# RG-LRU gates of a hybrid decoder layer: both gates of a block from one 64x128 stationary, in pairs on the row halves, with the turned prompt rows and a silu in other places

## What is computed

```
xc, conv_new = _causal_conv(xa, conv0, conv_w, conv_b)
xb = xc.reshape(B, L, N_BLK_A, BLK_A)                       # 8 blocks of 64
r = sigmoid(einsum('blnc,ncd->blnd', xb, wa).reshape(B, L, D_A) + ba)
i = sigmoid(einsum('blnc,ncd->blnd', xb, wx).reshape(B, L, D_A) + bx)
log_a = -8 * softplus(-lam) * r
u = sqrt(max(-expm1(2 * log_a), 0)) * (i * xc)
h = scan(h_t = exp(log_a) * h_{t-1} + u)
ya = h * silu(ga)
```

## Time and profile before

| | before |
|---|---|
| median of 3 runs | 942.91 us (942.79 to 1157.3) |
| the profiled execution: time | 940.88 us |
| its span, first to last instruction | 939.2 us |
| mean granted clock of TensorE | 0.985 of 2.4 GHz |
| PE busy | 872.4 us, 93% |
| DVE busy | 677.3 us, 72% |
| ACT busy | 511.4 us, 54% |
| POOL busy | 266.0 us, 28% |
| chain of work that ended last | PE 60%, DVE 18%, ACT 9%, issue 7%, POOL 3%, DMA 2% |

### The profile page before, as it was taken

One profiled execution on the slowest core, in us unless ns is written; L12 is line 12 of the kernel. 1 busy time (PEld: TensorE's weight loads), 2 busy tenths in 40 slices (PEclk: granted clock), 3 DMA queues, 4 the chain that ended last, 5 costly groups with the idle time before them and its releaser, 6 DMA issues.

```text
span 939.2 us, 20896 instructions
## 1 busy us (share of the span) xinstructions
PE 872.4 (93%) x8151; PEld 639.7 (68%) x8151; DVE 677.3 (72%) x1784; ACT 511.4 (54%) x1057; POOL 266.0 (28%) x348
## 2 busy tenths in 40 slices
PE   5788958999999999999999999999999999999884
PEld 4647847469665977588756866597757865686742
DVE  3577876757786887767785878678776778576865
ACT  2664658536663566547753566356653764346541
POOL 6041256503241223213140324122321314032400
PEclk9999988999999999999999999999999999999998
DMA  9975111301110102010110111010200001010414
GB/s 359 386 303 223 46 45 46 113 1 68 46 56 14 69 1 91 23 43 28 45 69 1 68 46 48 21 68 2 90 24 30 17 1 54 1 46 2 130 68 125
DMA packets 24703, 68.55 MB, mean 73 GB/s; under 512 B 3164, under 2 KB 12208, under 8 KB 20124
## 3 DMA queue, kind: packets, MB, share of 16 engines
q1 hardware_dynamic: 24604, 67.20, 19.7%
HBM read 56.24 MB, written 10.95 MB: 72 GB/s over the span
## 4 chain that ended last, share of the span: by engine, by line
PE 60%; DVE 18%; ACT 9%; issue 7%; POOL 3%; DMA 2%; SPq 0%; DVEq 0%; ACTq 0%; POOLq 0%
PE ring L450 48%; DVE xc L1392 6%; DMA work<-in_ada_w_dram 2%; DVE qlo L1295 2%; DVE kk L1313 2%; POOL wol L1807 2%; PE okv L547 1%; PE okv L549 1%; PE okv L548 1%; ACT wih L1059 1%; DVE qq L1311 1%; PE aux L569 1%; DVE xc L1390 1%; ACT qhi L939 1%; ACT L1002 1%
## 5 line engine op out<-in xcount | busy, mean ns | idle before, releaser
L450 PE MATMUL ring<-hnh,wih 128*128 128x256 bf16 (+1 forms) x1152 | 288.9, 262 | 2.2 <-DVE hnl L1440 2.2
L450 PE MATMUL ring<-hnl,wih 128*128 128x256 f16 (+1 forms) x1152 | 288.8, 262 | 0.0
L450 PE MATMUL ring<-hnh,wil 128*128 128x256 bf16 (+1 forms) x1152 | 288.8, 262 | 0.0
L450 PE MATMUL ring<-woh,work 128*128 128x512 f16 x512 | 164.7, 382 | 6.8 <-ACT sil L969 6.7
L1820 POOL TENSOR_TENSOR klo<-kk,khi 128x256 bf16<-128x256 f32 x96 | 75.5, 786 | 223.9 <-ACT khi L935 223.5
L450 PEld LDWEIGHTS ring<-hnh,wih 128*128 128x128 f16 x1152 | 109.9, 98 | 14.0 <-DVE hnl L1440 2.8
L450 PEld LDWEIGHTS ring<-hnl,wih 128*128 128x128 f16 x1152 | 109.8, 98 | 12.0
L450 PEld LDWEIGHTS ring<-hnh,wil 128*128 128x128 bf16 x1152 | 109.8, 98 | 11.6
L1295 DVE TENSOR_TENSOR qlo<-qq,qhi 128x256 f16<-128x256 f32 x112 | 66.6, 595 | 70.8 <-ACT qhi L939 61.3
L450 PE MATMUL ring<-wih,hnh 128*128 128x512 f16 x256 | 97.1, 379 | 2.4 <-ACT kk L918 1.3
L450 PE MATMUL ring<-wol,work 128*128 128x512 bf16 x256 | 97.7, 382 | 0.0
(11 more groups left out here) (366 smaller groups left out, 1899.5 us busy)
## 6 DMA issues: line engine op xcount, KB each, us to landing
work<-in_x_prompt_dram SPq DMA_DIRECT2D x16, 512.0 KB, 3.2
out_dram<-work SPq DMA_DIRECT2D x16, 512.0 KB, 2.6
xin<-in_x_turned_dram SPq DMA_DIRECT2D x7, 1024.0 KB, 4.8
xs<-in_x_prompt_dram SPq DMA_DIRECT2D x26, 256.0 KB, 3.8
work<-in_ada_w_dram SPq DMA_DIRECT2D x4, 1024.0 KB, 8.0
woh<-in_ada_w_dram SPq DMA_DIRECT2D x4, 1024.0 KB, 14.2
wol<-in_w_in_dram SPq DMA_DIRECT2D x4, 1024.0 KB, 13.6
work<-in_w_in_dram SPq DMA_DIRECT2D x4, 1024.0 KB, 10.3
```

What stands on the lines that cost most here:

```text
L450: last = mm(out, a(k), b(k), start=start and k == ks[0] and j == 0, stop=stop and k == ks[-1] and j == 2)
```

## The change

Both gates of a 64-channel block stand side by side in one 64x128 stationary: for the even block of a tile (rows 0 to 63) r left and i right, for the odd block (rows 64 to 127) i left and r right. A call of `gates` is four matmuls as before, of 64 rows each, neighbours on different row halves; the even blocks' results go to `aux[0]` and the odd blocks' to `aux[1]`, and one signal `g_ps` takes the place of two. There are no zeros left to write, so POOL's zeroing goes. Each sigmoid becomes two of 64 partitions; for i the source and the result lie on different partition halves. The decode's gates and sigmoids change in the same way. On PE the turned rows go behind the Q projection, the FR and Q projections wait for `esq` (the squares that free the ring banks) instead of the gate sigmoids, and `turn_k(n,1)` waits for the i sigmoids instead of the r ones. On ACT the second silu goes ahead of the root of half 0.

```
             def gates(n, p):
                 pe.wait_ge(cvc.sem, cvc.at(n, 8 * p + 8))
-                for w, s in ((0, gr_ps), (1, gi_ps)):
-                    ...
-                    for c in range(2):
-                        last = mm(aux[(1 + w + p) % 2][:, T * c:T * c + T], wg[:, w, 2 * p + c, :], xc[:, p, c, :],
-                                  start=True, stop=True)
-                    last.then_inc(s.sem, 1)
+                if p == 0:
+                    if n == 0:
+                        pe.wait_ge(wg_ld, 64)
+                        pe.wait_ge(gate_ok, 1)
+                    else:
+                        pe.wait_ge(ytl.sem, ytl.at(n - 1, 4))
+                else:
+                    pe.wait_ge(i_sig.sem, i_sig.at(n, 2))
+                if p == 0 and n < BODIES - 1:
+                    pe.wait_ge(xn_ok, NT + n + 1)
+                pe.wait_ge(kt_sb.sem, kt_sb.at(n, p + 1))
+                for c in range(2):
+                    for odd in range(2):
+                        k = slice(HALF * odd, HALF * odd + HALF)
+                        last = mm(aux[odd][:, T * c:T * c + T], wg[k, 2 * p + c, :], xc[k, p, c, :], start=True, stop=True)
+                last.then_inc(g_ps.sem, 1)
...
                 weights(1)
-                if not first:
-                    pe.wait_ge(i_sig.sem, i_sig.at(n - 1, 4))
+                if n == 1:
+                    pe.wait_ge(gp_sb, 2)
+                elif n > 1:
+                    pe.wait_ge(esq[0].sem, esq[0].at(n - 2, 2))
                 project(ring[0], FR, 0, n)
                 project(ring[0], FR, 1).then_inc(fr_ps.sem, 1)
+                weights(2)
+                if n > 1:
+                    pe.wait_ge(esq[1].sem, esq[1].at(n - 2, 2))
+                project(ring[1], Q_, 0)
+                project(ring[1], Q_, 1).then_inc(q_ps.sem, 1)
                 if not first:
                     turn_y(n - 1, 0)
                     turn_y(n - 1, 1)
-                weights(2)
-                project(ring[1], Q_, 0)
-                project(ring[1], Q_, 1).then_inc(q_ps.sem, 1)
...
             def gates_out(n, p):
-                act.wait_ge(gr_ps.sem, gr_ps.at(n, p + 1))
+                act.wait_ge(g_ps.sem, g_ps.at(n, p + 1))
                 act.wait_ge(iu.sem, iu.at(n, p))
                 for c in range(2):
-                    A(rr[:, c, :], aux[(1 + p) % 2][:, T * c:T * c + T], ACT.Sigmoid,
-                      bias=pcol("ba", 2 * p + c)).then_inc(r_sig.sem, 1)
-                act.wait_ge(gi_ps.sem, gi_ps.at(n, p + 1))
+                    for odd in range(2):
+                        k, src = slice(HALF * odd, HALF * odd + HALF), aux[odd][:, T * c:T * c + T]
+                        ins = A(rr[k, c, :], src[k, :], ACT.Sigmoid, bias=pcol("ba", 2 * p + c)[k, :])
+                    ins.then_inc(r_sig.sem, 1)
                 act.wait_ge(scan.sem, scan.at(n, 2 * p))
                 for c in range(2):
-                    A(ii[:, c, :], aux[p][:, T * c:T * c + T], ACT.Sigmoid, bias=pcol("bx", 2 * p + c)).then_inc(i_sig.sem, 1)
+                    for odd in range(2):
+                        k, o = slice(HALF * odd, HALF * odd + HALF), slice(HALF * (1 - odd), HALF * (1 - odd) + HALF)
+                        ins = A(ii[k, c, :], aux[odd][o, T * c:T * c + T], ACT.Sigmoid, bias=pcol("bx", 2 * p + c)[k, :])
+                    ins.then_inc(i_sig.sem, 1)
...
                 heads(n, 1, 7)
+                ga_out(n, 1)
                 root(n, 0)
-                ga_out(n, 1)
...
-            G.memset(wg[:, :, :, :], 0.0).then_inc(zeroed, 1)
```

More of the change, by code:

```diff
@@ L41 @@
 P = 128
+HALF = P // 2
 D = 1024
@@ L116, in build @@
         sil = sb("sil", [P, CT, T])
-        wg = sb("wg", [P, 2, CT, P])
+        wg = sb("wg", [P, CT, P])
         qq = sb("qq", [P, 2 * T])
@@ L184, in build @@
         u_ps = Signal("u_ps", 4)
-        gr_ps, gi_ps = Signal("gr_ps", 2), Signal("gi_ps", 2)
+        g_ps = Signal("g_ps", 2)
         f_sig, k_sig, q_sb = Signal("f_sig", 2), Signal("k_sig", 2), Signal("q_sb", 2)
@@ L367, in _ @@
                 if (kind, c) == ("ada", 7):
-                    sp.wait_ge(zeroed, 1)
                     for w, src in ((0, rg_wa), (1, rg_wx)):
@@ L371, in _ @@
                             v = src[0].rearrange("(t two) c d -> two c t d", two=2)[odd]
-                            sp.dma_start(wg[64 * odd:64 * odd + 64, w, :, 64 * odd:64 * odd + 64], v).then_inc(wg_ld, 16)
+                            col = HALF * (w ^ odd)
+                            sp.dma_start(wg[HALF * odd:HALF * odd + HALF, :, col:col + HALF], v).then_inc(wg_ld, 16)
             def residual_in(n, t):
@@ L503, in turn_y @@
                     pe.wait_ge(yb_ok.sem, yb_ok.at(n, 8))
-                    pe.wait_ge(r_sig.sem, r_sig.at(n, 4))
-                else:
                     pe.wait_ge(i_sig.sem, i_sig.at(n, 4))
@@ L553, in gates @@
                 pe.wait_ge(cvc.sem, cvc.at(n, 8 * p + 8))
-                for w, s in ((0, gr_ps), (1, gi_ps)):
[L555 to L565, removed]
-                    else:
-                        pe.wait_ge(i_sig.sem, i_sig.at(n, 2))
-                    for c in range(2):
-                        last = mm(aux[(1 + w + p) % 2][:, T * c:T * c + T], wg[:, w, 2 * p + c, :], xc[:, p, c, :],
-                                  start=True, stop=True)
-                    last.then_inc(s.sem, 1)
+                if p == 0:
+                    if n == 0:
+                        pe.wait_ge(wg_ld, 64)
+                        pe.wait_ge(gate_ok, 1)
+                    else:
+                        pe.wait_ge(ytl.sem, ytl.at(n - 1, 4))
[9 more added lines that the diff above has]
+                last.then_inc(g_ps.sem, 1)
             def ada(i, bank):
@@ L726, in body @@
                 if last_body:
-                    pe.wait_ge(r_sig.sem, r_sig.at(n, 2))
                     pe.wait_ge(i_sig.sem, i_sig.at(n, 2))
@@ L776, in _ @@
             turn_mod(3, ring[1], 0)
-            pe.wait_ge(zeroed, 3)
+            pe.wait_ge(zeroed, 2)
             pe.wait_ge(carry_zero, 2)
@@ L854, in _ @@
             pe.wait_ge(dv("conv_d"), 16)
[L855 to L858, removed]
+            for c in range(CT):
+                for hf in range(2):
+                    k = slice(HALF * hf, HALF * hf + HALF)
+                    last = mm((lev[1], aux[0])[hf][:, TD * c:TD * c + TD], wg[k, c, :], xcd[k, TD * c:TD * c + TD],
+                              start=True, stop=True)
             last.then_inc(dv("gates_ps"), 1)
@@ L1216, in _ @@
                 for c in range(CT):
-                    o = W4 * w + TD * c
-                    A(dst[:, TD * c:TD * c + TD], lev[1][:, o:o + TD], ACT.Sigmoid, bias=pcol(bias, c)).then_inc(dv("ri_d"), 1)
+                    cols = slice(TD * c, TD * c + TD)
+                    for hf in range(2):
+                        k, o = slice(HALF * hf, HALF * hf + HALF), HALF * (hf ^ w)
+                        ins = A(dst[k, cols], (lev[1], aux[0])[hf][o:o + HALF, cols], ACT.Sigmoid, bias=pcol(bias, c)[k, :])
+                    ins.then_inc(dv("ri_d"), 1)
             act.wait_ge(dv("ri_d"), 2 * CT)
@@ L1621, in _ @@
             rest(2)
-            dve.wait_ge(zeroed, 3)
+            dve.wait_ge(zeroed, 2)
             body(0, True, False)
```

## The result

The changed kernel takes 974.23 us (median of four runs, 970.93 to 977.17) against 942.85 us of the kernel before on the same chip. The ratio is 1.034, with a 95% interval of 1.030 to 1.038: slower, and outside the range of 932 to 957. The profiled execution took 977.17 us, its span is 975.5 us, and the mean granted clock of TensorE was 0.965 instead of 0.985.

The account below looks back on a forecast made before the run. It took a body's chain to run over TensorE, and over DVE and ACT in the last quarter. Body 0 to 1 +1.0, six bodies +3.0, last body and decode +1.5 sum to +5.5 us: 948.4, range 932 to 957.

Parts of the forecast that it names:

- Sigmoids on ACT: Gate sigmoids on ACT: eight halves start 0.36 us apart like whole ones, so a call grows 1.44 us; bounds 0 and 2.3.
- Rival E: Half sigmoids on ACT don't overlap: +2.3 us a call, level 0 at +1.4, 955 and up to 960 us; chance 0.07.
- Rival D: TensorE waits of about 2 us at level 7, over 1 at level 0 lower its clock: 966 us; chance 0.04.
- Level 7 is the first place that gives: Second pass's last level on TensorE, behind DVE's masked copy: 0.2 us slack, begins 1.35 us later, waits about 2 us.
- Level 0 is the second: Next body's first level on TensorE, behind DVE's `qrl`: 0.8 us slack, begins 0.5 us later each body, six times +3.0.
- The silu's wait goes for good: TensorE's wait for the second silu: 1.13 us goes with silu ahead of root, but level 7's +1.35 leaves +0.2.
- Gates in pairs run side by side: Gate matmuls on TensorE: 1.73 us a call becomes 0.87; saves 0.87, or about 0.67 with mode changes, lost in waits.
- Turned rows and looser waits cost nothing and gain nothing by themselves: Turned rows after Q and looser `esq` waits: no cost or gain; without them FR would wait for the longer sigmoids.
- The two ends: Body 0 to 1: +1.0 us. Last body and decode: +1.5 us together, +0.6 at decode input and +0.9 for sixteen sigmoids.

Follow-up runs that it names:

- pairs, grouped halves, rows ahead: Changed kernel with four half sigmoids writing partitions 0 to 63, then four writing 64 to 127, and ring[0]'s twelve output-row matmuls ahead of level 7: 961.27 us, ratio 1.020.
- the grouped halves: Changed kernel with only the half sigmoids reordered: four that write partitions 0 to 63, then four that write 64 to 127: 967.88 us, ratio 1.028.

## Why the prediction was wrong

The lengths of a middle body carry the account. The second column is the time from one call's first sigmoid to the instruction behind the last, the third the start of two level 0s that follow each other.

| kernel | sigmoids of a call | level 0 to level 0 | a body |
|---|---|---|---|
| before | 1.44 us | 579.76 to 681.75 | 101.99 us |
| + silu first | 1.44 | 574.73 to 675.43 | 100.70 |
| + turned rows behind Q | 1.44 | 574.54 to 675.22 | 100.68 |
| + pairs, whole sigmoids | 1.44 | 573.18 to 673.27 | 100.09 |
| pairs, halves all on one half | 2.87 | 586.39 to 688.74 | 102.35 |
| pairs, grouped halves, rows ahead | 3.38 | 588.64 to 692.44 | 103.80 |
| changed, clock at 1.00 | 3.92 | 711.22 to 816.09 | 104.87 |
| changed, clock falls | 3.92 | 604.83 to 711.22 | 106.39 |

From 101.99 to 106.39: -1.29 for the silu, -0.02 for the turned rows, -0.59 for the pairs, +4.78 for the halves, +1.52 for the clock. Behind level 7 the clock falls in five of the six middle bodies, at 1.5 to 1.7 us each. In the profiled execution, whose span is 36.3 us longer than before, the six bodies take 28.7 us more: six times 2.88 = 17.3 for the halves less the gains, about 8.2 for these five falls, 1.7 for one more behind level 0 of body 1, and 1.5 in the body from 390.22 to 498.30, where ACT waits 1.56 us for a DMA (at 405.35). The rest is 3.7 us ahead of them and 4.0 behind. The halves alone (4.78 a body) turn the gain of the other parts (1.90 a body) into a loss of 2.9.

**The step that failed: "Sigmoids on ACT", the +1.44 a call.** It measured +2.48, above the upper bound of 2.3 too, because each half starts some 0.02 us after the end of the one before it. The prediction argued from the earlier trace rows that partitions count for nothing, which is right for the duration (0.47 us on 64 partitions as on 128), and then took the spacing of whole sigmoids from the earlier trace rows for halves as well. But the spacing is another quantity than the duration, and it was the one that mattered. The trace of before did hold a hint: the three instructions on 8, 4 and 3 partitions of the earlier trace rows stand in one row of ACT's timeline of the kernel before.

```profile
919.87 1.47 ACT L1236 ACTIVATE wil<-okv 8x512 f32<-8x512 f32 x3
```

1.47 us for durations of 569, 268 and 587 ns, 1.42 in sum: they don't overlap at all, where the whole ones of the earlier trace rows do. They start at partitions 0, 32 and 64, so like the halves they change partitions from one to the next; the first two lie in the same half, so a change of half is not the only one that can go with a lost overlap. By that row the upper bound of 2.3 was the nearest one. The Trainium skill, "ScalarE: Activation LUTs", What ACT_TABLE_LOAD costs, says that ACTIVATEs that follow each other overlap by about 93 ns, without a condition. The whole sigmoids agree (0.47 long, 0.36 apart); the halves that change sides do not (0.49 apart), and the measurement decides.

With this term at its predicted size, the rest of the sum nearly comes out: the kernel whose halves do start 0.36 apart takes 949.1 us where 948.4 was predicted, and a body 102.35 where 102.5 was. Against the kernel before beside it (941.56) that is +7.6 where +5.5 was predicted; 2.4 of it stand ahead of the first level 0 (107.72 instead of 105.31), before any gate has run.

**Rival E had the size and still fell short.** It named 2.3 a call and put level 0 at +1.4 and the time at 955 to 960. Without the clock level 0 is at 104.87 - 101.99 = +2.9. It let only the second call's extra reach level 0. In the runs both calls' extra does: what the first adds, less the silu's 1.13, goes through level 7, the output rows and the turned keys into the second call's gates. From 2.87 to 3.92 us a call the body grew by 2.52, a bit more than twice the 1.05. The instruction behind a call starts later too: from `xa` to the head copy behind it are 0.62 us (563.60 to 564.22), where they are 0.48 with all halves on one half (548.33 to 548.80).

**Rival D's mechanism came in on top.** Its condition was a wait of about 2 us at level 7 and one of over 1 us at level 0 in every body; they are 2.77 and 1.18. Its price of 2.5 us a body was somewhat high: 1.5 to 1.7. That "the rows say that 2.3 is not yet enough" rested on one row, and does not hold: at the same place, level 0 of body 1, TensorE waits 2.29 us in the kernel before and in the kernel with the silu first, and the granted clock behind it is 1.00 in the one and 0.70 in the other (wait until 170.25, window 171.8 to 176.0). Of the ten profiles in which TensorE waits 2.29 to 2.31 us there, the clock falls in eight.

**What was right.**

- *Level 7 is the first place that gives.* It waits for DVE's masked copy, 1.74 us with the predicted spacing (about 2 was said), 2.77 with the real one. One reading was off: most of the 0.2 us ahead of it was called signalling, but where TensorE does wait, level 7 begins 0.06 us after the copy (572.05 to 572.11), so most was slack. It moves the sum by no more than 0.1 a body.
- *Level 0 is the second.* 0.67 and 1.18 us of waiting for `qrl`, where "1 us or more" was said.
- *The silu's wait goes for good.* No middle body waits for it in the changed kernel. But its worth was undersized as soon as nothing takes it back: 1.29 us a body and 9.9 us in all, more than the 6.7 us of waits in the earlier trace rows.
- *Gates in pairs run side by side.* 1.14 us a call against 1.73: 0.59 saved, near the 0.67 that the rows gave with an entry and a leaving of 0.1 each, and not the 0.87 of two full lanes. The rule of the Trainium skill, "TensorEngine Tiling (Array Packing)", Tiling Modes, that a change of mode drains TensorE, goes in that direction; no run here separates the drain. With whole sigmoids 0.59 us of two calls' 1.2 reach the body's end. That with halves the saved time is waited away, as predicted, no run shows: with the clock at 1.00 a body takes 390.64 - 283.71 = 106.93 us with half sigmoids in the kernel before and 106.22 in the changed kernel with the silu behind the root, 0.71 less for pairs, turned rows and looser waits together.
- *Turned rows and looser waits cost nothing and gain nothing by themselves* as long as the sigmoids are whole, and without them FR waits for the longer sigmoids (1.51 us, the half sigmoids in the kernel before).

**The two ends were undersized in the same way as the bodies.** From level 0 of body 0 to that of body 1 the changed kernel takes 3.3 us more (175.48 - 105.68 against 171.79 - 105.31), where +1.0 was taken. For the tail, two of the sixteen decode half sigmoids, ACT's timeline of the changed kernel:

```profile
930.29 0.28 ACT L1225 ACTIVATE xin<-lev,par 64x32 f32<-64x32 f32 x1
930.59 0.28 ACT L1225 ACTIVATE xin<-aux,par 64x32 f32<-64x32 f32 x1
```

They start 0.30 apart, the last at 934.83: 4.8 us for the sixteen instead of 1.53 for eight, +3.3 where +1.5 was taken.

What stays open is when a wait lowers the clock. In the profiles here waits of 0.34 to 1.76 us in middle bodies were never followed by a clock below 1.00, those of 2.77 us were in nine of twelve bodies (five of six in the changed kernel, four of six with the silu back), those of 2.57 us with the grouped halves in five of six, those of 2.44 us with the half sigmoids in the kernel before in four of six, and those of 2.0 us ahead of IV in three of six. Nothing that I looked at told the bodies with a fall from those without.

## What to carry to other kernels

The price of an instruction on an engine that works through a queue is the distance from its start to the next start, not its duration; read it from a row of *several* in sequence, and from one whose partitions change as they will in the new code. Saving on TensorE by a layout that makes another engine handle halves pays only if that engine has room on the path: here 0.6 us a call was bought with 2.5 us of ACT. When one part of a combined change gives a gain by itself (the silu, one line, 1.1%), it is worth taking alone.

## What the runs showed of the hardware

In these runs two ACTIVATEs on 64 partitions and 256 columns overlap by 0.11 us if both read the same half and both write the same half (0.36 apart), and not at all if the source's or the result's half changes between them (0.47 to 0.49 apart); the PSUM bank and the result tile may change without harm. On 32 columns the sixteen halves of the decode take 0.30 us each (4.8 us), the eight whole sigmoids 0.19 (1.53 us).

The same stall can be had as a wait or as a slow clock: with the silu behind the root a body took 106.2 us both where TensorE waited 1.25 us for it and where the clock of 0.50 had already made TensorE that late. The wait's disappearance from the list of waits was there no gain.
